# One of two modulation blocks weighed by GpSimd, beside VectorE, in a fused two-layer transformer kernel

## The reference

```python
cond = jax.nn.silu(c)
for l in range(DEPTH):                                     # 2
    mod = jnp.einsum('bd,de->be', cond, w_ada[l]) + b_ada[l]
    sh1, sc1, g1, sh2, sc2, g2, sh3, sc3, g3 = split(mod, 9)
    h = rms_norm(x, norm_ffn1[l]) * (1 + sc1) + sh1
    x = x + 0.5 * g1 * swiglu(h, w_gate1[l], w_up1[l], w_down1[l])    # d_ff = 2816
    h = rms_norm(x, norm_mix[l]) * (1 + sc2) + sh2
    x = x + g2 * token_mixing(h, ...)                      # three kinds of attention
    h = rms_norm(x, norm_ffn2[l]) * (1 + sc3) + sh3
    x = x + 0.5 * g3 * swiglu(h, w_gate2[l], w_up2[l], w_down2[l])
```

## Time and profile before

| | us |
|---|---|
| median of 3 runs | 1189.13 (1187.82 to 1190.16) |
| the profiled execution | 1189.2 |
| its span | 1187.5 |
| PE busy | 1148.7 (97%) |
| DVE busy | 873.1 (74%) |
| ACT busy | 525.9 (44%) |
| POOL busy | 64.6 (5%), nearly all of it issuing DMAs |

### The profile page before, as it was taken

One profiled execution on the slowest core, in us unless ns is written; L12 is line 12 of the kernel. 1 busy time (PEld: TensorE's weight loads), 2 busy tenths in 40 slices (PEclk: granted clock), 3 DMA queues, 4 the chain that ended last, 5 costly groups with the idle time before them and its releaser, 6 DMA issues.

```text
span 1187.5 us, 20427 instructions
## 1 busy us (share of the span) xinstructions
PE 1148.7 (97%) x7940; PEld 1046.7 (88%) x7940; DVE 873.1 (74%) x1294; ACT 525.9 (44%) x665; POOL 64.6 (5%) x79
## 2 busy tenths in 40 slices
PE   6999999999999999999999999999999998999998
PEld 6889999989898699999978999998989876999996
DVE  7788888778766877766777887888787588645545
ACT  2334334445566533443353344335356555433432
POOL 2011101100000000000001011000000000000000
PEclk9899999989999999999989999999999999999999
DMA  9889998945511667778846988994733244665551
GB/s 305 266 298 304 307 325 304 310 145 178 177 55 54 213 212 249 240 236 264 265 143 213 330 301 296 309 353 152 250 114 101 72 164 159 209 212 188 166 194 72
DMA packets 160369, 258.35 MB, mean 218 GB/s; under 512 B 8366, under 2 KB 127278, under 8 KB 160320
## 3 DMA queue, kind: packets, MB, share of 16 engines
q1 hardware_dynamic: 140739, 182.25, 46.7%
q0 software_dynamic: 19584, 75.50, 19.0%
HBM read 256.56 MB, written 1.05 MB: 217 GB/s over the span
## 4 chain that ended last, share of the span: by engine, by line
PE 75%; DVE 13%; ACT 3%; DMA 3%; DVEq 3%; issue 2%; POOL 0%; ACTq 0%; POOLq 0%
PE bank L1145 15%; PE bank L1146 15%; PE bank L1147 15%; PE bank L1225 7%; PE bank L1221 7%; PE bank L1222 7%; DVE wlo L764 3%; DMA ada<-in_w_ada_dram 3%; DVE room L722 3%; PE bank L1422 2%; PE bank L1163 1%; PE bank L1341 1%; DVE acc L722 1%; ACT whi L438 1%; DVEq L724 1%
## 5 line engine op out<-in xcount | busy, mean ns | idle before, releaser
L438 ACT ACTIVATE whi<-raw 128x2048 fp32r<-128x2048 f32 (+1 forms) x174 | 321.6, 1850 | 25.8 <-DMA raw<-in_w_gate_dram 14.7
L764 DVE TENSOR_TENSOR wlo<-raw,whi 128x2048 fp32r<-128x2048 f32 (+2 forms) x130 | 281.5, 2197 | 22.9 <-ACT whi L438 21.8
L1145 PE MATMUL bank<-hhi,whi 128*128 128x256 f32 (+1 forms) x1008 | 287.7, 285 | 0.0
L1146 PE MATMUL bank<-hlo,whi 128*128 128x256 f32 (+1 forms) x1008 | 285.6, 283 | 0.0
L1147 PE MATMUL bank<-hhi,wlo 128*128 128x256 f32 (+1 forms) x1008 | 285.5, 283 | 0.0
L1145 PEld LDWEIGHTS bank<-hhi,whi 128*128 128x128 f32 (+1 forms) x1008 | 193.1, 192 | 2.4 <-issue 2.0
L1146 PEld LDWEIGHTS bank<-hlo,whi 128*128 128x128 f32 (+1 forms) x1008 | 193.2, 192 | 0.5 <-issue 0.5
L1147 PEld LDWEIGHTS bank<-hhi,wlo 128*128 128x128 f32 (+1 forms) x1008 | 193.1, 192 | 0.0
L481 ACT ACTIVATE eb<-bank 128x512 f32<-128x512 f32 x44 | 26.3, 598 | 362.2 <-PE bank L1225 362.2
L722 DVE SCALAR_TENSOR_TENSOR room<-ada,cT,room 128x512 f32 (+3 forms) x266 | 170.1, 639 | 20.2
L1221 PE MATMUL bank<-hhi,whi 128*128 128x256 f32 x736 | 180.2, 283 | 0.0
(11 more groups left out here) (198 smaller groups left out, 1375.0 us busy)
## 6 DMA issues: line engine op xcount, KB each, us to landing
ada<-in_w_ada_dram POOLq DMA_DIRECT2D x68, 1024.0 KB, 5.8
raw<-in_w_gate_dram SPq DMA_DIRECT2D x44, 1024.0 KB, 6.0
raw<-in_w_up_dram SPq DMA_DIRECT2D x44, 1024.0 KB, 6.8
raw<-in_w_down_dram SPq DMA_DIRECT2D x44, 1024.0 KB, 6.0
raw<-in_w_in_dram SPq DMA_DIRECT2D x28, 1024.0 KB, 5.7
raw<-in_w_out_dram SPq DMA_DIRECT2D x8, 512.0 KB, 3.3
raw<-in_w_out_dram SPq DMA_DIRECT2D x4, 1024.0 KB, 5.7
LG<-in_b_ada_dram SPq DMA_DIRECT2D x6, 512.0 KB, 8.3
```

Of the source, the lines that this page charges most:

```text
L438: last = act.activation(dst, src, ACT.Copy)
L764: last = dve.tensor_tensor(dst, src, hi.bitcast(F32), ALU.subtract)
L1145: pe.matmul(ps, l_hi, r_hi, start=first, stop=False)
L1146: pe.matmul(ps, l_hi, r_lo, start=False, stop=False)
```

## The change

DVE weighs slot 0 alone in FFN1. GpSimd weighs slot 1: 8 multiplications by a column of `cT`, written over the block itself, then sums of halves (1024, 512, 256 columns), the last of them into `room`. It does so between the fills that it issues, so the refill of both slots stands behind its weighing in its queue, slot 1 first. Its loop over steps is written out. A new semaphore `odd_ready` counts its blocks, and TensorE waits for it before it reads them. GpSimd's first weighing of a layer waits for `modc_done`, that is until TensorE has read what `room` held before.

```diff
+            def weigh_odd(l, i):
+                pool.wait_ge(ada_full[1], (i + ada_turn(l, 1, 1)) * 16)
+                sums = held[:, at_cols(i * (2 * CW) + CW, CW)]
+                for k in range(KT):
+                    pool.tensor_scalar(ada[:, 1, k, :], ada[:, 1, k, :], cT[:, k:k + 1], None, ALU.mult)
+                for half in (4, 2, 1):
+                    pool.drain()
+                    dst = sums.unsqueeze(1) if half == 1 else ada[:, 1, 0:half, :]
+                    last = pool.tensor_tensor(dst, ada[:, 1, 0:half, :], ada[:, 1, half:2 * half, :], ALU.add)
+                last.then_inc(odd_ready, 1)
+                pool.drain().then_inc(ada_used[1], 1)
...
-                with pool.Fori(0, NF) as i:
-                    for k in range(2):
-                        fill(k, ada_turn(l, k, i + 1), bass.ds(rows_l, KT), bass.ds(i * (2 * CW) + (AHEAD + k) * CW, CW))
+                def two(i):
+                    for k in (1, 0):
+                        m = AHEAD + 2 * i + k
+                        fill(k, ada_turn(l, k, i + 1), bass.ds(rows_l, KT), slice(m * CW, (m + 1) * CW))
+                for k in range(2):
+                    fill(k, ada_turn(l, k, 1), bass.ds(rows_l, KT), slice((AHEAD + k) * CW, (AHEAD + k + 1) * CW))
+                pool.wait_ge(modc_done, MODC_PRE + nth(l, MODC_L, 0))
+                for i in range(NF):
+                    weigh_odd(l, i)
+                    if i + 1 < NF:
+                        two(i + 1)
...
                 if which == 0:
-                    weigh_ada([i + ada_turn(l, k, 1) for k in range(2)], [0, 1],
-                              held[:, at_cols(i * (2 * CW), 2 * CW)].rearrange("p (a n) -> p a n", a=2))
+                    weigh_ada([i + ada_turn(l, 0, 1)], [0], held[:, at_cols(i * (2 * CW), CW)].rearrange("p (a n) -> p a n", a=1))
...
                 pe.wait_ge(acc_ready, nth(l, ACC_L, ACC_PRE + (2, NF, NF + MID + 3)[n]))
+                if n < 2:
+                    pe.wait_ge(odd_ready, nth(l, NF, (2, NF)[n]))
...
+                pe.wait_ge(odd_ready, nth(l, NF, 6))
                 sum_held(nth(l, ACC_L, ACC_PRE + 6), D, 2 * KT, PS[6])
```

More of the change, by code:

```diff
@@ L188, in build @@
         acc_ready = sem("acc_ready")
+        odd_ready = sem("odd_ready")
         modc_done = sem("modc_done")
```

## The result

The changed kernel took 1299.6 us (median of 4 runs, 1294.88 to 1302.59) beside 1189.64 us for the kernel before. The ratio is 1.0932, with a 95% interval of 1.0902 to 1.0962. The sign was as forecast, the size (110 us in place of 29) was not, and the time lies outside the range of 1183 to 1245.

The account below looks back on a forecast made before the run. TensorE was taken to bound the steady FFN1 step at 17.1 us. Engines taking turns would cost 18 steps x 1.5 = 27 us, plus 2 at the layer's start: +29 on 1189.2 is 1218 us, range 1183 to 1245.

Parts of the forecast that it names:

- What bounds the kernel: FFN1: TensorE, busy 97% of the span, sets the 17.1 us steady step; a shorter DVE weighing only adds idle time.
- GpSimd's work: GpSimd's scalings and sums per FFN1 step: 4.5 to 9.3 us, taken as 6.9.
- the budget of 9.4: Longest GpSimd weighing that still fits an FFN1 step: 17.1 - 0.88 - 6.8 = 9.4 us.
- The fills behind the weighing: GpSimd's queue in FFN1: weighing, refills and landing make a round of 14.6 us, under the 17.1 us step.
- The two engines at SBUF: FFN1: DVE and GpSimd taking turns give a middle round of 18.6 us, 1.5 over the step; chance 0.57.
- rival 3: FFN1: GpSimd's weighing alone takes over 9.4 us with DVE untouched; at 11 us, 1213 us in all; chance 0.08.
- The gain: TensorE's waits for late DVE in the first steps of both layers and layer 0's last step go: 5.4 us.
- The layer's start: GpSimd's first weighing of a layer gets before short DVE instructions on the chain: 2 us lost.
- the gate's cover: TensorE's wait for odd blocks before spreading layer 0's gate: thirteen us of cover, so free.

Follow-up runs that it names:

- e2: The changed kernel with GpSimd doing only 4 of the 8 scalings and the sums of 512 and 256 columns, half of each odd block left out: 1191.4 us, ratio 1.001.
- e3: The changed kernel with DVE's own refills (slot 0) of FFN1 issued from ACT's queue, GpSimd's work and slot 1's refill unchanged: 1315.4 us, ratio 1.104.
- e1: The changed kernel with GpSimd's 11 arithmetic instructions a step replaced by seven memsets that read nothing: 1286.8 us, ratio 1.080.
- e7: The changed kernel with a second buffer for the odd blocks, so that GpSimd weighs one while the next lands: 1262.0 us, ratio 1.0624.
- e5: The kernel before, plus four GpSimd scalings of 128x256 a step that feed nothing, behind the two refills: 1188.1 us, ratio 0.998.
- e6: The kernel before, with GpSimd weighing only the second block of layer 1's first FFN1 step: 1191.3 us, ratio 1.0005.
- e8: The changed kernel with a second buffer for the odd blocks and one 128x2048 product in place of GpSimd's eight scalings: 1288.2 us, ratio 1.0852.

## Why the prediction was wrong

*What bounds the kernel* was right: a steady FFN1 step is TensorE's 17.1 us, and a shorter weighing on DVE is worth nothing in it: e2, with DVE relieved and GpSimd in time, gave a ratio of 1.001.

*GpSimd's work* is the step that failed. "Upper bound, a pass for each operand read or written: a scaling 2 passes, 0.55 us" was no bound. A scaling took 0.92 us undisturbed, so eight took 7.2 us where the bound had 4.4 and the sum 2.7 to 4.4. The sums were inside their bounds: 2.3, 1.3 and 0.7 us, 4.3 in all with a bound of 4.9 (4.53 + 0.35). Own length: 12.05 us with the waits between (e3's last round), not 6.9, over the upper end of 9.3 and over the budget of 9.4 that the prediction itself had worked out. An iota writes without reading, and from it nothing follows for an instruction that reads; the "passes" had no row behind them. The estimate from the Trainium skill's GPSIMD Engine Reference, 3.1, 2.2 ns a column for a two-input sum, agrees with the run: 2.34 us for 1024 columns is 2.3 ns. It was the scalings at the iota's rate, laid beside it, that made 6.6 us. This one term carries the miss: with 12.05 us for 6.9 the prediction's own sum gives a round of 12.05 + 3.4 + 0.88 + 6.8 = 23.1 us, 6.0 over the step, 18 x 6.0 + 2 = 110 us. That this is the measured loss to the microsecond is luck: the stretch was 2.9, not 3.4, and the rounds over the step were some 20, not 18.

*The fills behind the weighing* was the right mechanism, and near in size. The round was forecast as W + 0.88 + 6.8, that is 7.7 us behind the weighing; measured 8.0 in the mean (8.97 in the round shown). Slot 1's refill goes first, so the 0.88 us of the other is not in its round; the 0.62 us of drain and semaphore is, and was left out. In the round shown the landing took 8.35 us (median of layer 0's FFN1 refills 8.3), longer than the 6.8 of the earlier trace rows; in others it was about 5.9.

*The two engines at SBUF* was right as a mechanism and too large in its share. They do exclude each other (e1 beside the changed kernel). In the changed kernel it adds 2.9 us to a weighing in the mean (14.9 for 12.05; 1.6 in the round shown), where 3.4 to 4.6 was forecast; DVE stands idle for much of the round. The loop hid the rest of it, which came out where the loop was opened: 6.0 us in e3's busy rounds. It was given 0.57 of the chance and rival 3, GpSimd alone too slow, 0.08. By the shares worked out at e3 each made about half of the loss. What rival 3 asks for, W alone over 9.4 us, came true with 12.05; its "DVE untouched" did not (L901 2157 ns for 1225). Those 0.57 alone were the right answer only for e7, with its opened loop.

*The gain* of 5.4 us was too large. Of it, 2.8 to 3.3 us rested on what was most likely a slow landing of one execution (e5, e6). The first step of layer 0 was shortened as forecast, from 18.62 us (55.82 to 74.44 in the profile before) to 17.26 in e2 (57.31 to 74.57), and e2's next step lost 4.1 us again, which more than cancels it. The rows name the cause: DVE's refill stands behind GpSimd's first weighing (52.26 to 62.24, nearly 10 us beside DVE's), and DVE waits 4.75 us for its block, until 74.42.

*The layer's start* (2 us) and *the gate's cover* were not tested apart. The gate's wait was free in the changed kernel, and not in e3.

## What to carry to other kernels

Before work goes to an engine that also issues a loop's refills, write down its round (own length, drain, issues, landing), add the stretch by a busy neighbour (here a quarter in the closed loop, 12 to 15 us, and a half with the loop open, 12 to 18), and compare it with the step. Where no row of the trace shows an operation, another operation of the same engine is no bound for it: a single run with it in an idle place, as e5, would have given the 0.92 us. Beside a DVE with two-input instructions, one long read of GpSimd did more harm than eight short ones (e8 against e7); how much of that was its place in the step stays open.

## What the runs showed of the hardware

- GpSimd, fp32 in SBUF, undisturbed: scaling of 128x256 0.92 us with a column as factor, 0.84 with a constant; 2.5 ns a column; two-input sum of 1024 columns 2.34 us, of 256 columns 0.73.
- GpSimd's reads and DVE's two-input instructions exclude each other, here for a whole instruction: a half split of 1.23 us, begun 0.36 us behind a product of 2048 columns of 3.62 us, took 4.35 (e8), the rest of the product and then its own length. Against a busy DVE it is GpSimd that is stretched: four scalings 8.4 us for 3.6 (e2), a weighing 18.0 for 12.05 (e3).
- Beside GpSimd's writes only one DVE instruction grew: the first one of the weighing, a tensor_scalar with one SBUF input, 1.98 us in the mean for 0.35 in e1, beside a memset of 1.81 us.
- TensorE's granted clock was 0.88 of its 2.4 GHz in the mean over the changed kernel's first FFN1 (44 to 240 us), where it was 0.99 before; TensorE stood waiting there for up to 11.7 us at a time. GpSimd set the step there, so nothing shows that the clock cost time by itself.
